# Routing of a mixture of experts moved into the attention phase, with only the sample tile's own part behind it

## The reference, cut to what matters

```python
h = h + memory_attn(rmsnorm(h, g_mem_q), mem_k, mem_v, w_mq, w_mo)
hn = rmsnorm(h, g_ffn).reshape(B * T, D)
# hier_route: gl = 4 group logits, el = 8 expert logits of the chosen group
gsel = argmax(gl); top_p, top_i = top_k(softmax(el), 2)
comb = softmax(gl)[gsel] * top_p / sum(top_p)
eid  = gsel * 8 + top_i                      # two of 32 experts for each row
# routed_experts: rows sorted by expert, in blocks of 128 rows of one expert
h = silu(x @ w_gate[e]) * (x @ w_up[e]);  y = h @ w_down[e]
out = h + sum over the row's two experts of comb * y
```

## Time and profile before

| | us |
|---|---|
| median of three runs (2022.0 to 2030.35) | 2027.47 |
| the profiled execution, its own time | 2033.57 |
| its span in the trace | 2031.7 |
| busy in the span: PE, DVE, ACT, POOL | 1823.7, 1186.7, 820.9, 337.5 |

### The profile page before, as it was taken

How to read it: one execution, slowest core, us unless ns; L and a number is a source line. 1 busy time by engine, 2 the same in 40 slices (tenths; PEclk the granted TensorE clock), 3 DMA queues, 4 the chain that set the end, 5 groups by cost and what they waited for, 6 DMA issues and landing times. The chain is left out here.

```text
span 2031.7 us, 35586 instructions
## 1 busy us (share of the span) xinstructions
PE 1823.7 (90%) x14874; PEld 1494.7 (74%) x14874; DVE 1186.7 (58%) x1311; ACT 820.9 (40%) x934; POOL 337.5 (17%) x307
## 2 busy tenths in 40 slices
PE   7999997888988895899999998836999999999995
PEld 7998885777777764688788886325888888888872
DVE  4544102677777566513333323047899999999974
ACT  5111212344444313402221211005777777778763
POOL 1322002234333330000000000001111111111105
PEclk9999998999999877899999998966999999999998
DMA  7755244222222208653011105336999999999987
GB/s 280 247 191 181 104 140 122 67 72 73 83 83 78 80 2 279 230 207 125 32 53 38 58 32 217 157 153 252 387 402 405 404 407 403 404 407 403 403 311 284
DMA packets 111973, 419.12 MB, mean 206 GB/s; under 512 B 25892, under 2 KB 44264, under 8 KB 82920
## 3 DMA queue, kind: packets, MB, share of 16 engines
q1 hardware_dynamic: 99592, 373.76, 49.4%
q0 software_dynamic: 7072, 25.69, 3.4%
q10 hardware_dynamic: 5184, 17.82, 2.2%
HBM read 350.10 MB, written 75.53 MB: 209 GB/s over the span
## 5 line engine op out<-in xcount | busy, mean ns | idle before, releaser
L2607 DVE TENSOR_TENSOR ex_wd_lo<-moe_raw,ex_wd_hi 128x2048 fp32r<-128x2048 f32 x62 | 141.8, 2289 | 48.6 <-ACT ex_wd_hi L2718 48.6
L2607 DVE TENSOR_TENSOR ex_wg_lo<-moe_raw,ex_wg_hi 128x2048 fp32r<-128x2048 f32 x66 | 148.4, 2286 | 15.3 <-ACT ex_wg_hi L2718 15.3
L2718 ACT CAST ex_wg_hi<-moe_raw 128x2048 fp32r<-128x2048 f32 x66 | 125.9, 1908 | 55.1 <-PE banks L2500 25.6
L2607 DVE TENSOR_TENSOR ex_wu_lo<-moe_raw,ex_wu_hi 128x2048 fp32r<-128x2048 f32 x64 | 143.7, 2285 | 0.7 <-ACT ex_wu_hi L2718 0.6
L2718 ACT CAST ex_wd_hi<-moe_raw 128x2048 fp32r<-128x2048 f32 x62 | 118.5, 1913 | 43.2 <-PE banks L2500 24.9
L2718 ACT CAST ex_wu_hi<-moe_raw 128x2048 fp32r<-128x2048 f32 x64 | 122.5, 1915 | 31.4 <-PE banks L2500 31.4
L516 PE MATMUL banks<-pj_w_hi,pj_x_hi 128*128 128x448 f32 (+1 forms) x288 | 109.9, 381 | 11.3 <-DVE pj_x_lo L347 11.3
L2500 PE MATMUL banks<-ex_wg_hi,ex_x_hi 128*128 128x512 f32 x256 | 105.2, 411 | 12.7 <-issue 5.9
L516 PE MATMUL banks<-pj_w_lo,pj_x_hi 128*128 128x448 f32 (+1 forms) x288 | 109.6, 380 | 0.0
L2500 PE MATMUL banks<-ex_wu_hi,ex_x_hi 128*128 128x512 f32 x256 | 102.7, 401 | 0.0
L2500 PE MATMUL banks<-ex_wg_hi,ex_x_lo 128*128 128x512 f32 x256 | 101.8, 398 | 0.0
(11 more groups left out here) (429 smaller groups left out, 4572.5 us busy)
## 6 DMA issues: line engine op xcount, KB each, us to landing
moe_raw<-w_e_gate SPq DMA_DIRECT2D x64, 1024.0 KB, 7.8
moe_raw<-w_e_up SPq DMA_DIRECT2D x64, 1024.0 KB, 7.4
moe_raw<-w_e_down SPq DMA_DIRECT2D x64, 1024.0 KB, 7.4
blocks<-ex_y ACTq DMA_DIRECT2D x32, 512.0 KB, 7.6
mx_pin<-proj SPq DMA_DIRECT2D x8, 1664.0 KB, 7.0
h<-at_h SPq DMA_DIRECT2D x18, 512.0 KB, 2.7
at_slots<-cache_mem_k SPq DMA_DIRECT2D x8, 1024.0 KB, 11.8
at_slots<-cache_mem_v SPq DMA_DIRECT2D x8, 1024.0 KB, 7.0
```

The costliest lines, as they stand in the source:

```text
L2607: v.tensor_tensor(w_lo(w), raw[:, j], as_f32(w_hi(w)), ALU.subtract).then_inc(S_("w_split"), 1)
L2718: act.copy(w_hi(home(j, n)), raw[:, j]).then_inc(S_("w_high"), 1)
```

## The change

`phase_route` is gone. Its work lies in three places.

- In `phase_attention`, the logits stay on the chip (L has nine tiles) and `store_lg` is gone. SP loads the four tables before the sample's keys. DVE does `prompt_choices` between `logits(7)` and the sample's maxima, and `prompt_places` between the copy of the sample's probabilities and the split of its outputs; ACT has two small exponentials; PE does `prompt_ranks` in front of the values and the 16 prompt products of the table in three parts of 5, 5 and 6 beside `turn_outputs`. Behind the sample's `logits` come `sample_places` on DVE, `sample_ranks` and two table products on PE and two exponentials on ACT. The table has 32 columns, those of the blocks that are always there. SP loads expert 0's weights when the last values are used.
- In `phase_experts`, the overflow starts, the destinations and the overflow list are made from the counts, ranks and choices: `over_starts`, `corrections` and `destinations` in DVE's list of the last expert, where `hidden_of` now stands before `low(4)`; `over_lists` and 18 products only in the body of an overflow block. Each engine's loop waits for `n_over`, POOL's gathers of results also for `dest`. SP loads two small tables at the start, and loads rows 4 to 7 of h behind the last down pieces.
- Buffers lie elsewhere: `moe_raw` is inside the space of the sample's keys and values, and the split weights, y1 and y2 move.

Cut to its core:

```diff
@@ attention, SP
-                    if i >= 1:
-                        store_lg(i - 1)
                     if i == NT - 2:
                         sp.wait_ge(S_("queried"), TILES)
+                        for dst, src in ((strict[:], d["upper"]), (cnt_c[:], d["count"]), (valid[:], d["valid"]), (token[:], d["token"])):
+                            sp.dma_start(dst, src).then_inc(S_("tables"), 16)
...
+                sp.wait_ge(S_("os_done"), 2)
+                for j in range(len(PIECES)):
+                    sp.dma_start(raw[:, j], expert_piece(d, j, 0)).then_inc(S_("weights"), 16)
@@ attention, DVE
                 logits(NT - 1)
+                prompt_choices()
                 maxima(NT, 2, 6)
                 divide(NT, 2)
                 v.wait_ge(S_("p_turned"), TILES)
                 v.tensor_copy(bT[:, 0:4, :], PS[:, 0, :].rearrange("p (c t) -> p c t", t=P)).then_inc(S_("pT"), 1)
+                prompt_places()
...
                 logits(NT)
+                sample_places()
@@ attention, DVE, new: one tile's choice; sample_places cut
+                def pick_one(dst, src, best, t, n, scale=None):
+                    top = s[:, 11, NT:TILES]
+                    lk(red(best, src, AX.X, ALU.max))
+                    lk(v.scalar_tensor_tensor(t, src, best, desc[:, 0:n], ALU.is_equal, ALU.mult))
+                    lk(red(top, t, AX.X, ALU.max))
+                    if scale is None:
+                        return v.tensor_scalar(dst, t, top, None, ALU.is_equal)
+                    return v.tensor_scalar(dst, t, top, scale, ALU.is_equal, ALU.mult)
+                def sample_places():
...
+                    v.wait_ge(S_("ranks"), 2)
+                    b = PS[:, RANKS, NT * NE:TILES * NE]
+                    for k in range(2):
+                        ins = tt(tmp[:, k, NT], b, O_(k, NT), ALU.mult)
+                    lk(ins)
+                    lk(red(rank[:, :, NT:TILES], tmp[:, :, NT:TILES], AX.X, ALU.add))
+                    for k in range(2):
+                        v.tensor_scalar(at_slot[:, k * TILES + NT], slot_no, rank[:, k, NT:TILES], None, ALU.is_equal).then_inc(S_("placed"), 1)
...
+                    v.wait_ge(S_("exps_s"), 1)
+                    weights(slice(NT, TILES), tg[:, NT:TILES])
+                    v.wait_ge(S_("table"), 1)
+                    v.tensor_copy(slot_tok[:], PS[:, TABLE, 0:NE])
@@ attention, PE
                 ins.then_inc(S_("p_turned"), 1)
+                prompt_ranks()
                 pe.wait_ge(S_("pT"), TILES)
                 for b in range(4):
                     ins = sample_values(b)
                 ins.then_inc(S_("os_done"), 1)
+                pe.wait_ge(S_("placed"), 4)
+                table(prompt_pairs[0:5])
                 turn_outputs(0)
                 for b in range(4, DB):
                     ins = sample_values(b)
                 ins.then_inc(S_("os_done"), 1)
+                table(prompt_pairs[5:10])
                 turn_outputs(1)
+                table(prompt_pairs[10:16])
                 attend(NT)
                 turn_hn(NT)
                 router(NT)
+                sample_ranks()
+                pe.wait_ge(S_("placed"), 8)
+                table(sample_pairs).then_inc(S_("table"), 1)
@@ experts, SP
-                for j in GU:
+                for j in (0, 1):
                     sp.wait_ge(S_("w_split"), done_gu(LAST, j))
                     load_rows((2 * j, 2 * j + 1))
                 load_dn(NE - 1)
+                sp.wait_ge(S_("w_split"), done_gu(LAST, 3))
+                load_rows(range(4, 8))
@@ experts, DVE, last step
                     if final:
+                        over_starts(c0, c1)
+                        hidden_of(n, done_gu(n, 3))
                         low(4, done_dn(n, 4), n)
-                        hidden_of(n, done_gu(n, 3))
+                        corrections()
                         hidden_low(n)
                         low(5, done_dn(n, 5), n)
+                        destinations()
                         return
@@ experts, every engine's loop over overflow blocks; PE's body
+            eng.wait_ge(S_("n_over"), 1)
+            n_blocks = eng.value_load(n_over[0:1, 0:1], min_val=0, max_val=NOVER)
             with eng.Fori(0, NOVER) as j:
-                with eng.If(j < n_over):
+                with eng.If(j < n_blocks):
                     body(j)
...
+                    for i in range(PAIRS):
+                        ins = pe.matmul(PS[:, OVER_TABLE, 0:NOVER], over_at[:, i, :], of_over[:, i, :], start=i == 0, stop=i == PAIRS - 1)
```

More of the change, by code:

```diff
@@ L2404, in _ @@
                 sp.dma_start(ident[:], d["ident"]).then_inc(S_("ident"), 16)
+                sp.dma_start(cnt_c[:], d["count"]).then_inc(S_("tables"), 16)
+                sp.dma_start(token[:], d["token"]).then_inc(S_("tables"), 16)
                 for j in range(NP):
@@ new lines, in over_starts @@
+                def over_starts(c0, c1):
+                    v.wait_ge(S_("tables"), 32)
+                    lk(tt(nbt, bc(counts.unsqueeze(2), NE, 8), bc(full.unsqueeze(1), NE, 8), ALU.is_gt))
+                    lk(red(nb, nbt, AX.X, ALU.add))
+                    lk(v.tensor_copy(c0, nb))
+                    step = 1
+                    while step < NE:
+                        v.tensor_copy(c1[:, 0:step], c0[:, 0:step])
+                        lk(tt(c1[:, step:NE], c0[:, step:NE], c0[:, 0:NE - step], ALU.add))
+                        c0, c1, step = c1, c0, 2 * step
+                    v.tensor_copy(n_over[:], c0[:, NE - 1:NE]).then_inc(S_("n_over"), 1)
+                    lk(tt(start, c0, nb, ALU.subtract))
+                    lk(v.tensor_scalar(corr, start, float(CAP), float(NE * CAP - CAP), ALU.mult, ALU.add))
+                    lk(tt(corr, corr, ebase, ALU.subtract))
```

401 lines of the change are left out of this document (219 added, 182 removed).

## The result

| | before | after |
|---|---|---|
| median, us | 2027.99 (2022.0 to 2030.35) | 1999.26 (1997.67 to 2002.25, 4 runs) |
| ratio | | 0.9862, interval 0.9846 to 0.9878 |
| the profiled execution, its own time | 2033.57 | 1998.08 |
| its span | 2031.7 | 1996.3 |

The change saves 28.7 us, 1.4%. The prediction was 1996.2 in a range of 1989 to 2005, with 0.97 for faster by more than half a per cent: the sign, the size and the range hold, and the point is 3.1 us too low: 2.6 of it because less was saved than the 31.3 predicted, 0.5 because the median before is 2027.99 and not the 2027.47 of the first three runs.

The account below looks back on a forecast made before the run. Routing was taken as a serial stretch of 36.8 us on the path to the first expert. Savings of 28.1 - 0.3 + 3.5 = 31.3 us from a median of 2027.47 gave 1996.2 us, range 1989 to 2005.

Parts of the forecast that it names:

- Term 1: Routing behind the sample: 36.8 us go, the sample's part and one hand-over come back, 28.1 us saved.
- the hand-over: From the end of the sample's routing to POOL's first expert instruction: taken as 1.6 us.
- the marks: DVE's marks M in the sample's routing, input to PE's rank product: reached after 3.7 us.
- Rival (b): Sample's routing dearer, with longer waits and hand-over, late ranks and choices: 7.7 us less gained, 2003.9 us; chance 0.09.
- Term 2: Routing work put beside the sample's attention: mostly hidden, ranks 1.0 us late, clock gives 0.7; 0.3 us lost.
- rival (c): Filled seams in the sample's attention bring PE's clock back, for output product and ranks: 1994.9 us; chance 0.16.
- Term 3: Last expert: PE's stall before `turn_last` gone, 1.9 us, and low clock behind it, 1.6: 3.5 us saved.
- Rival (d): Expert loop slower from moved buffers, DVE's splits setting the step: 2029 us and more; chance 0.03, shared with no effect.
- Rival (a): Tail gains nothing, through DVE's new instructions or PE's longer empty-block loop body: 1999.7 to 2001 us; chance 0.14.

Follow-up runs that it names:

- e0: The kernel before, unchanged, timed against itself: median 2027.89 us against 2028.81, ratio 0.9999.
- e5: The kernel before with only `hidden_of` put ahead of `low(4)` in DVE's last expert: 2022.63 us, a single execution.
- e3: The changed kernel with `low(4)` back ahead of `hidden_of` on DVE, SP's new order kept: 2001.46 us, a single execution.
- e4: The changed kernel with SP's old order back (rows 4 to 7 of h ahead of the last down pieces): 2002.08 us, a single execution.
- e9: The changed kernel with the places of the split up and split down weights exchanged: 2001.10 us, a single execution.
- e7: The changed kernel with unread products filling PE's idle time around the sample's routing and first expert, identity kept loaded: 1992.6 us, ratio 0.9836.
- f4: e7 with f3's buffer places: 1991.39 us, ratio 0.9825.
- f1: The changed kernel once more, unchanged, traced again: 1997.73 us, a single execution.
- f3: The changed kernel with the expert phase's small buffers at their old relative places (64 bytes of padding, allocations reordered): 1996.03 us, a single execution.

## Why the prediction was right, and where not

**Term 1, 28.1 predicted, 28.0 measured.** The sample's part was put at 7.1 and took 7.46, the hand-over at 1.6 and took 1.36. To the marks it was 4.15 for 3.7, since the steps with a scalar from a buffer last 0.22 to 0.29 and not 0.19; through PE 0.72 for 0.85; behind it 2.59 for 2.5. Rival (b) is out.

**Term 2, 0.3 lost predicted, 2.6 gained in after's trace (1.1 where the output product starts low).** This is the mis-sized term. Its work was hidden as predicted: tables 0.73, 0.73 and 0.82 in the seams, choices with 2.81 of idle time left (2.7 predicted), places done in time. The ranks did make the values 1.1 us late (1.0 predicted). But I credited the clock only with half of 1.4 at the output product, and missed the values: with PE busy through the ranks the clock is up from 1292.9 and the first half takes 8.96 in place of 11.27; the output product's 1.4 then came in full in this trace. The row was there, 0.52 for 5.25 us; rival (c) named it and took 0.6 for it where 2.3 came. The price of the ranks was misread from the same row: 5.2/8 = 0.65 us for one pass of 512 columns, where the first four of these products start 0.85 us apart. The four passes of 256 columns took 0.43 each, 1.7 together and not 1.3; that all of the ranks took 2.1 (2.2 predicted) is in part luck.

**Term 3, 3.5 predicted, 3.5 between the two first traces, 1.6 between the others.** The stall (1.9 in before, 1.63 in e0) is gone, and e5 shows that DVE's order alone does it. The 1.6 of clock were read as a certain consequence of the stall; e0 has the stall and no low clock. SP's order, to which the term gave nothing of its own, would have done the same alone (e3).

**The expert loop, nothing predicted, 1.9 lost.** Rival (d) looked in the right place, at buffers that lie elsewhere, and on the wrong engine: DVE's splits are 2281 to 2288 ns as before, and PE's down products are further apart. It had been priced at 32 us with a threshold and nothing below, so a small loss was in no term.

**The empty loops.** PE's final sum starts 14.3 us behind its last product in after as in before. Rival (a) is out for this kernel: neither the body's length nor the new instructions on DVE cost anything. But in e4, e9, e7 and f4 PE's idle time before that sum was 17.4, 17.6, 16.8 and 16.3, and the last column of the table is 1.2 to 3.6 us longer. The row in after and in e9:
```profile
1963.50 3.75 PE L2632 MATMUL banks<-moe_h_rows,ex_ident 128*128 128x512 f32 x4 [14.30 <-issue]
```
```profile
1966.20 3.75 PE L2632 MATMUL banks<-moe_h_rows,ex_ident 128*128 128x512 f32 x4 [17.60 <-issue]
```
The loop's own line shows where the time is, as in the earlier trace rows: after, f1 and e9:
```profile
L2399 PEldq MOVE  x17: 29/29/40, 1951.2 to 1962.8; - x17
L2399 ACTq MOVE  x17: 3/29/34, 1951.4 to 1961.5; - x17
```
```profile
L2399 ACTq MOVE  x17: 29/29/34, 1951.0 to 1957.7; - x17
```
```profile
L2399 PEldq MOVE  x17: 29/29/696, 1950.6 to 1964.5; - x17
```
Most of the excess lies in one or two turns of the loop: 1.70 and 2.15 us in e9, 2.83 in e4, 2.15 in e7, 1.04 and 1.46 in f4, where a turn on PE takes some 0.74. The rest, some 0.9, lies between the last turn and the sum (1.7 us in e9, 0.7 in after). ACT's and SP's loops have such turns too, 1.45 and 2.13 us on ACT in after, and in f1, the same program, none. So on these two engines they come and go between executions. For PE no program was traced with both values, so whether its longer loop is of the program stays open; e9 has the same instructions as after, with other addresses in them. What the engines wait for in such a turn stays open too. The Trainium skill (Advanced Engine Details and Errata, "ISA Cache") gives TensorE a larger instruction store than the others (128 KB where they have 32), which I had left out at rival (a); no run here shows a store of any size.

**The sum.** The terms as measured behind tile 7's logits: 28.0 + 2.4 + 2.5 - 1.9 - 0.1 = 30.9 between the means of the two traces of before and of after (the last is the end). That is near the 31.3 predicted, by errors of opposite sign: 2.7 too little in term 2, 1.0 too much in term 3, 2.0 for the loop and the end. So that it came out so near is in part luck. The time came out 3.1 us later than predicted. I subtracted terms of one execution, with its own low clock of 1.6, from a median that need not have it; and traces of after's variants have the lower clock now and then (1.4 at the output product, 1.2 at the first expert), which after's timed runs may have too. Both are argued, not shown.

## What to carry to other kernels

A serial stretch of small instructions is worth moving nearly whole: its price behind the last input is that of one tile, about 0.2 us an instruction, and can be added up beforehand. When work is put in front of a product on an idle engine, price the clock of what follows as well as the delay, and look at more than one trace: less than 0.2 us in when the clock rose went with 1.4 us later on. And a program that moves buffers should be compared step by step in its longest loop: 0.07 us a step is easily passed over and was 2 us here.

## What the runs showed of the hardware

- The pitch of fp32r products of 512 columns depends on where buffers lie: 226 to 232 or 231 to 238 ns, by the pair of products, with the same instructions and full clock (2.4 GHz), from a shift of 64 bytes and an order of allocation (f3 against after).
- With the seams ahead of it filled, the output product ran at full clock in five traces and had 3.4 us at the lower level (1.2 GHz) in five. In the former the clock had risen 0.11 us or more behind the start of the values, in the latter just before it.
- A loop over 16 empty blocks costs POOL 6.7, DVE 8.1 and PE 11.6 us. Single turns of it took 1.0 to 2.8 us on PE in four of 12 programs. On ACT and SP such turns were there in one execution of after (ACT 10.1 us in all) and not in the other (6.7), for no cause found.
